# Two linear-attention mixers: elementwise work given to GpSimd, the second substitution put between the first merges, the last grams one step early

## The chip, the cores and the metric

The kernel runs on one core of a Trainium2 chip. The metric is the device time of one execution, in microseconds. Before the change the median of three runs is 3515.9 us (3514.63 to 3524.79).

## What is computed

Two transformer blocks of two layers each, on one sequence of 512 tokens of width 1024, in fp32. Each layer of the first block has a feed-forward part, a mixer and another feed-forward part. The mixer splits one projection into sparse attention, an RWKV-7 recurrence (4 heads of 64) and a gated delta rule (4 heads of 64). The change lies in the last two. The delta rule in its chunked form, which fixes the order of its work:

```python
decay = jnp.exp(jnp.where(incl, g[..., :, None] - g[..., None, :], -jnp.inf))
kb = k * beta[..., None]
lower = jnp.where(strict, jnp.einsum('bhncd,bhnsd->bhncs', kb, k) * decay, 0.0)
rhs = jnp.concatenate([v * beta[..., None], kb * jnp.exp(g)[..., None]], axis=-1)
sol = lax.linalg.triangular_solve(jnp.eye(C) + lower, rhs, left_side=True, lower=True, unit_diagonal=True)
# per chunk, with u, wk = the halves of sol and intra = the masked q k^T * decay
v_new = uc - wc @ S
o = (qc * exp(gc)) @ S + ac @ v_new
S = S * exp(g_last) + (kc * exp(g_last - gc)).T @ v_new
```

The RWKV recurrence is brought to the same form: a unit lower triangular matrix per block and head is inverted, then the state is carried from block to block.

## The kernel before

Everything is written out by hand, engine by engine, with semaphores. Weights come as 128x1024 tiles over a ring of four (SyncE loads them; ScalarE rounds a tile to its high part, line 738; GpSimd makes the low part by four subtractions of 128x256, line 695; TensorE multiplies in three passes, lines 2231 to 2233). GpSimd does nothing else but this, in the order of the tiles (`low_parts`, line 698), apart from a cast near the end.

The mixer, once per layer (`recurrences` of each engine): 512 tokens are four blocks (TB = 4) of 128. In a block, four heads of RWKV and four of the delta rule lie side by side, so a matrix per head and block is a tile of 2 units x 512 columns (1024 columns). It goes as follows.

1. Under the attention of the same layer, VectorE and ScalarE prepare gates, decays and the convolution. Its end is the start of what matters here. VectorE adds the decay mask to four blocks of four heads (line 1755, 16 instructions), ScalarE takes SiLU and squares of keys and queries (lines 1044, 1045), TensorE sums the squares (line 2378), ScalarE takes roots (929), VectorE inverts and widens them (1539, 1541), and TensorE spreads them over the partitions (2385). Ten and then five matmuls of 128 columns without use (2519, 2524) stand around the sums.
2. VectorE scales the keys (1804) and multiplies them by beta (1805), TensorE makes the first block's grams (2640), and VectorE masks them (`take_grams`, 1835 and 1836). Then VectorE finishes the attention output (1775), v times beta (1815), the small diagonal blocks (`small_blocks`, 1847 to 1850) and the query scaling (1818). TensorE turns ten units (2604), and ScalarE copies them out (1076).
3. The inverse. VectorE inverts the 16x16 diagonal blocks by substitution: 15 steps of three dependent instructions, a shuffle and two tensor_tensor (lines 1859 to 1861), on 8 to 120 columns. `lower_corners` (1866) cuts out the part of the matrix for the first merge, `spread_inverses` (1873 to 1878) lays the small inverses out. TensorE and VectorE or ScalarE then merge 16 to 32, 32 to 64 and 64 to 128 (levels 4, 5, 6; TensorE lines 2677, 2679, 2689, 2691, 2695; `merge16` on VectorE, 1892 and 1893).
4. `core_step(l, n)` for n = 0 to 4 does the merges of block n and the recurrence of block n-1: grams with the state's inputs (`a_grams`, 2640, masked in 1903 to 1907), right sides R (2716 to 2722), new values U by the inverse (`writes`, 2731), outputs and the new state (2738 to 2758; `next_state` on VectorE, 1917 to 1923). VectorE runs the substitution of block n+1 in step n, after the merges at level 4 of block n:

```python
                if n < TB:
                    dve.wait_ge(S["small_ready"], b + 1)
                    for g in range(2):
                        merge16(g)
                if n + 1 < TB:
                    lower_corners(n + 1)
                    substitute(range(15, 0, -1))
                    spread_inverses(l, n + 1)
                if 0 < n < TB:
                    next_state()
```

Each engine's queue is in order, so a waiting instruction holds everything behind it. TensorE's order in a step is: gram n+1, level 4 products, `a_grams`, level 4 inverse products, level 5 products, right sides, and so on. After step 4 `post` goes on with the output projection, for which four weight tiles are ready since before the mixer.

## Time and profile before

| | |
|---|---|
| runs (3) | 3515.9 us median, 3514.63 to 3524.79 |
| the profiled execution | 3516.75 us, its span 3514.9 us |
| busy in the span | TensorE 96%, VectorE 41%, ScalarE 36%, GpSimd 48% |
| mean granted clock of TensorE | 0.981 |
| GpSimd idle in the mixers | 564 to 783 us and 1728 to 1954 us |
| first mixer's core | from 615 us (attention's end) to 770 us (output projection) |
| second mixer's core | from 1786 us to 1940 us |

Of the rows below, a timeline row is: start and length in us, engine, line, operation, output and inputs, shape, number of merged instructions, and in brackets the idle time before it with what ended it. A row of windows is: stretch and length, busy time (with the number of instructions) of TensorE, its weight loads, VectorE, ScalarE and GpSimd, then TensorE's granted clock, DMA share and GB/s. Lines are those of the kernel before.

### The profile page before, as it was taken

How to read it: one execution, taken by the hardware profiler on the slowest of the kernel's cores; microseconds unless marked ns; L12 is line 12 of the kernel's file. 1: busy time of each engine (PE TensorE's matmuls, PEld its weight loads, DVE VectorE, ACT ScalarE, POOL GpSimd, SP SyncE). 2: the span in 40 equal slices, each digit the busy share in tenths (PEclk: the TensorE clock that was granted, in tenths of full speed). 3: DMA queues.
4: the chain of work that ended last, by engine and by line, in shares of the span. 5: the costliest groups of instructions: out<-in, count | busy, mean ns of one | idle time of the engine just before them, and what ended most of it. 6: DMA issues, size and time to landing. Idle time of an engine off the chain costs nothing.

```text
span 3514.9 us, 47288 instructions
## 1 busy us (share of the span) xinstructions
PE 3377.4 (96%) x16952; PEld 2779.3 (79%) x16952; DVE 1430.3 (41%) x2753; ACT 1254.3 (36%) x1892; POOL 1674.2 (48%) x2052
## 2 busy tenths in 40 slices
PE   7999998799999999999969999999899999999999
PEld 6888776688888888887658888878667888888887
DVE  5431597845221422148786522224563110341100
ACT  4222436424222322234553432233533332433321
POOL 6765552005665566655300366644304555435554
PEclk9999999899999999999989999999999999999999
DMA  5443321003443344333100244332102222212222
GB/s 184 143 144 112 106 94 60 2 7 132 143 143 114 125 143 144 123 104 96 61 25 2 87 146 144 131 103 84 66 1 84 95 95 96 78 61 102 98 99 96
DMA packets 104224, 340.50 MB, mean 97 GB/s; under 512 B 12144, under 2 KB 17936, under 8 KB 103968
## 3 DMA queue, kind: packets, MB, share of 16 engines
q1 hardware_dynamic: 87824, 283.08, 24.2%
q10 hardware_dynamic: 16272, 55.65, 4.8%
q8 instruction: 88, 1.44, 0.2%
q14 instruction: 40, 0.33, 0.0%
HBM read 330.78 MB, written 2.65 MB: 95 GB/s over the span
## 4 chain that ended last, share of the span: by engine, by line
issue 38%; POOL 33%; PE 27%; DVE 1%; POOLq 0%; ACT 0%; DMA 0%; SPq 0%; DVEq 0%
POOL w_lo L695 33%; PE ps L2233 7%; PE ps L2231 7%; PE ps L2232 7%; PE ps L3003 1%; PE ps L2982 1%; PE ps L2254 0%; PE ps L2991 0%; PE ps L2255 0%; PE ps L2259 0%; PE ps L3093 0%; DVE stat L2132 0%; DVE sq L2125 0%; PE ps L3099 0%; PE ps L2983 0%
## 5 line engine op out<-in xcount | busy, mean ns | idle before, releaser
L695 POOL TENSOR_TENSOR w_lo<-w_raw,w_hi 128x256 fp32r<-128x256 f32 x2040 | 1667.5, 849 | 1823.2 <-ACT w_hi L738 1817.0
L2231 PE MATMUL ps<-h_hi,w_hi 128*128 128x512 f32 x2608 | 1020.7, 391 | 0.9 <-ACT mem L955 0.9
L2233 PE MATMUL ps<-h_hi,w_lo 128*128 128x512 f32 x2608 | 1016.3, 390 | 0.0
L2232 PE MATMUL ps<-h_lo,w_hi 128*128 128x512 f32 x2608 | 1015.9, 390 | 0.0
L738 ACT ACTIVATE w_hi<-w_raw 128x1024 fp32r<-128x1024 f32 x510 | 538.5, 1058 | 916.8 <-DMA w_raw<-in_tiles 916.5
L2231 PEld LDWEIGHTS ps<-h_hi,w_hi 128*128 128x128 f32 x2608 | 490.0, 188 | 112.8 <-issue 6.1
L2233 PEld LDWEIGHTS ps<-h_hi,w_lo 128*128 128x128 f32 x2608 | 490.0, 188 | 102.6
L2232 PEld LDWEIGHTS ps<-h_lo,w_hi 128*128 128x128 f32 x2608 | 490.2, 188 | 100.6
L2232 PE MATMUL ps<-a_lo,w_hi 128*128 (+1 forms) x1120 | 437.2, 390 | 0.0
L2231 PE MATMUL ps<-a_hi,w_hi 128*128 (+1 forms) x1056 | 411.0, 389 | 0.0
L2233 PE MATMUL ps<-a_hi,w_lo 128*128 (+1 forms) x1056 | 411.0, 389 | 0.0
L881 ACT ACTIVATE sil<-ps 128x512 f32<-128x512 f32 x128 | 76.5, 598 | 694.5 <-PE ps L2233 686.3
L1474 DVE TENSOR_TENSOR sil<-sil,ps 128x512 f32<-128x512 f32 x128 | 88.0, 688 | 530.5 <-ACT sil L881 530.5
L1476 DVE TENSOR_TENSOR a_lo<-sil,a_hi 128x512 f32 (+1 forms) x132 | 93.9, 711 | 495.2 <-ACT a_hi L889 495.2
L2232 PEld LDWEIGHTS ps<-a_lo,w_hi 128*128 128x128 f32 x1120 | 211.1, 188 | 43.9
L2231 PEld LDWEIGHTS ps<-a_hi,w_hi 128*128 128x128 f32 x1056 | 198.3, 188 | 41.2
L2233 PEld LDWEIGHTS ps<-a_hi,w_lo 128*128 128x128 f32 x1056 | 198.2, 188 | 40.9
L1453 DVE SCALAR_TENSOR_TENSOR ada_raw<-ada_raw,sq 128x1024 f32<-128x1024 f32 x96 | 164.8, 1720 | 11.1 <-DMA ada_raw<-in_ada_tiles 11.1
L1507 DVE SCALAR_TENSOR_TENSOR x<-ps,x 128x512 f32<-128x512 f32 x32 | 22.1, 692 | 311.5 <-PE ps L2233 311.0
L1507 DVE SCALAR_TENSOR_TENSOR x<-ps,ada,x 128x512 f32<-128x512 f32 x16 | 12.0, 751 | 193.3 <-PE ps L2233 193.2
L889 ACT ACTIVATE a_hi<-sil 128x512 f32 (+1 forms) x132 | 81.2, 615 | 1.6 <-DVE sil L1471 1.6
L2254 PE MATMUL ps<-h_hi,w_hi 128*128 128x512 f32 x176 | 72.1, 410 | 5.1 <-ACT h_hi L839 5.1
(470 smaller groups left out, 3616.9 us busy)
## 6 DMA issues: line engine op xcount, KB each, us to landing
w_raw<-in_tiles SPq DMA_DIRECT2D x510, 512.0 KB, 3.3
ada_raw<-in_ada_tiles ACTq DMA_DIRECT2D x96, 512.0 KB, 3.3
mem<-mem SPq DMA_DIRECT2D x80, 64.0 KB, 2.1
x<-in_x_t SPq DMA_DIRECT2D x2, 1024.0 KB, 6.5
sq<-in_cond ACTq DMA_DIRECT2D x4, 512.0 KB, 4.0
mem<-gates SPq DMA_DIRECT2D x8, 256.0 KB, 3.8
consts<-in_consts SPq DMA_DIRECT2D x1, 1280.0 KB, 12.7
core_mem<-gates SPq DMA_DIRECT2D x8, 128.0 KB, 2.9
```

The costliest lines, as they stand in the source:

```text
L695: ins = nc.gpsimd.tensor_tensor(w_lo[:, s, part], w_raw[:, s, part], w_hi[:, s, part].bitcast(F32), ALU.subtract)
L738: nc.scalar.activation(w_hi[:, t % RING, :], w_raw[:, t % RING, :], ACT.Copy).then_inc(S["w_hi_ready"], 1)
L881: nc.scalar.activation(sil[:, j, :], ps[:, 2 * j, :], ACT.Silu).then_inc(S["silu_ready"], 1)
L889: nc.scalar.activation(a_hi[:, 2 * i + j, :], sil[:, j, :], ACT.Copy).then_inc(S["a_hi_ready"], 1)
L1453: nc.vector.scalar_tensor_tensor(raw, raw, 1.0, cond_rows(n)[0], ALU.mult, ALU.mult, accum_out=ada[:, 0, column]).then_inc(S["ada_used"], 1)
L1474: nc.vector.tensor_tensor(sil[:, j, :], sil[:, j, :], ps[:, 2 * j + 1, :], ALU.mult).then_inc(S["af_ready"], 1)
L1476: nc.vector.tensor_tensor(a_lo[:, 2 * i + j, :], sil[:, j, :], a_hi[:, 2 * i + j, :].bitcast(F32), ALU.subtract).then_inc(S["a_ready"], 1)
L2231: nc.tensor.matmul(bank, wh, hi, start=first, stop=False, skip_group_check=True)
L2232: nc.tensor.matmul(bank, wh, lo, start=False, stop=False, skip_group_check=True)
L2233: return nc.tensor.matmul(bank, wl, hi, start=False, stop=last, skip_group_check=True)
L2254: nc.tensor.matmul(ps[:, banks[r], :], w_hi[:, slot, block], h_hi[:, k, :], start=(n == 0), stop=False, skip_group_check=True)
L2982: nc.tensor.matmul(ps[:, 2 * (i % 2), :], q, kmla[0:QKD, h, 0:T], start=True, stop=True)
```

## The change

GpSimd gets, per layer, in `delta_parts`: the decay masks of blocks 1 to 3 (two adds of 128x512 each; block 0 stays on VectorE), keys times decay, v times beta, the query scaling, queries and keys times the decay factor (with a separate negation), and `lower_corners` of all four blocks (each 128x1024). This stands in its queue between the low part of the last tile loaded ahead of the mixer and that of the next. ScalarE gives the squares to VectorE, splits its exponential in two and copies the spread query factors out of PSUM, scaled. TensorE's head sums move behind the attention's last products, and the five matmuls of line 2524 go. The two halves of the spread inverses are signalled apart. In step 0, VectorE runs six steps of block 1's substitution, then the first merge, one step, the second merge, eight steps. The masking of the small blocks is rearranged so that it works on half as many columns. The grams of the last block's recurrence move: two of them into step 3, two behind the right sides of step 4.

```diff
+            def delta_parts(l):
+
+                pool.wait_ge(S["g_taken"], l + 1)
+                pool.wait_ge(S["dt_spread"], 64 * (l + 1))
+                for n in range(1, TB):
+                    at = ST_GNEG + 4 * n
+                    decay = mem[:, 20 + n, :].rearrange("p (a b t) -> p a b t", a=2, b=2)
+                    g = stat[:, at:at + 4].rearrange("p (b a) -> p a b", b=2).unsqueeze(3).to_broadcast([P, 2, 2, P])
+                    nc.gpsimd.tensor_tensor(heads(mem[:, 20 + n, :]), heads(mem[:, 20 + n, :]), over_heads(const("decay_neg")), ALU.add).then_inc(S["gdn_parts"], 1)
+                    pool.wait_ge(S["gdn_parts"], 10 * l + 2 * n - 1)
+                    nc.gpsimd.tensor_tensor(decay, decay, g, ALU.add).then_inc(S["gdn_parts"], 1)
+                pool.wait_ge(S["spread_taken"], 3 * l + 3)
+                pool.wait_ge(S["eg_ready"], 4 * l + 2)
+                nc.gpsimd.tensor_tensor(mem[:, 24:26, :], mem[:, U_KG:U_KG + 2, :], mem[:, U_DELTA:U_DELTA + 2, :], ALU.mult).then_inc(S["gdn_parts"], 1)
+                pool.wait_ge(S["conv_act_v"], 3 * l + 3)
+                nc.gpsimd.tensor_tensor(mem[:, 37:39, :], mem[:, 37:39, :], core_mem[:, R_SQ:R_SQ + 2, :], ALU.mult).then_inc(S["gdn_parts"], 1)
+                lower_corners(l, 0)
+                pool.wait_ge(S["turned_out"], 11 * l + 1)
+                q = mem[:, U_QG:U_QG + 2, :]
+                nc.gpsimd.tensor_tensor(q, q, sil[:, :, :], ALU.mult).then_inc(S["gdn_parts"], 1)
+                pool.wait_ge(S["turned"], 11 * (l + 1))
+                pool.wait_ge(S["gdn_parts"], 10 * l + 9)
+                eg, qe, kbe = (mem[:, u:u + 2, :] for u in (41, 37, 24))
+                nc.gpsimd.tensor_tensor(qe, q, eg, ALU.mult)
+                nc.gpsimd.tensor_scalar(kbe, mem[:, 39:41, :], -1.0, None, ALU.mult).then_inc(S["gdn_parts"], 1)
+                pool.wait_ge(S["gdn_parts"], 10 * l + 10)
+                nc.gpsimd.tensor_tensor(kbe, kbe, eg, ALU.mult).then_inc(S["gdn_ready"], 1)
+                for n in range(1, TB):
+                    lower_corners(l, n)
+
+            def lower_corners(l, n):
+
+                b = TB * l + n
+                pool.wait_ge(S["gram_taken"], 2 * b + 2)
+                if n == 0:
+                    pool.wait_ge(S["gdn_parts"], 10 * l + 8)
+                else:
+                    pool.wait_ge(S["dx_ready"], merge_turn(b - 1, 4, 1) + 1)
+                nc.gpsimd.tensor_tensor(all_heads(core_mem[:, C_N:C_N + 2, :]), all_heads(lower_units(n)), const("levels").unsqueeze(1).to_broadcast([P, 8, P]), ALU.mult).then_inc(S["corners_ready"], 1)
+
...
+                ahead = BASE[f"mix_out{l}"] + RING
+                low_parts(done, ahead)
+                delta_parts(l)
+                done = ahead
...
-                        for at, unit in ((2, U_KG), (0, U_QG)):
-                            link(nc.scalar.activation(mem[:, unit:unit + 2, :], core_mem[:, G_CONV + at:G_CONV + at + 2, :], ACT.Silu))
-                            nc.scalar.activation(mem[:, U_NORMED + at:U_NORMED + at + 2, :], mem[:, unit:unit + 2, :], ACT.Square).then_inc(S["head_sq"], 1)
-                        load_sqrt()
-                        head_roots(2, 2, 1.0, EPS_NORM, 2)
+                        nc.scalar.activation(mem[:, U_KG:U_KG + 2, :], core_mem[:, G_CONV + 2:G_CONV + 4, :], ACT.Silu).then_inc(S["conv_act_v"], 1)
...
+                nc.scalar.activation(mem[:, U_QG:U_QG + 2, :], core_mem[:, G_CONV:G_CONV + 2, :], ACT.Silu).then_inc(S["conv_act_v"], 1)
+                load_sqrt()
+                head_roots(2, 2, 1.0, EPS_NORM, 2)
+                factors_out()
                 head_roots(3, 2, 1.0, EPS_NORM)
                 act.wait_ge(S["spread_taken"], 3 * l + 2)
-                nc.scalar.activation(mem[:, 20:24, :], mem[:, 20:24, :], ACT.Exp).then_inc(S["dt_ready"], 1)
+                nc.scalar.activation(mem[:, 20, :], mem[:, 20, :], ACT.Exp).then_inc(S["eg_ready"], 1)
+                act.wait_ge(S["gdn_parts"], 10 * l + 6)
+                nc.scalar.activation(mem[:, 21:24, :], mem[:, 21:24, :], ACT.Exp).then_inc(S["eg_ready"], 1)
...
+                act.wait_ge(S["turned"], due("turned"))
+                nc.scalar.activation(sil[:, :, :], ps[:, 2:4, :], ACT.Copy, scale=HD ** -0.5).then_inc(S["turned_out"], 1)
...
+                for h in range(4):
+                    block = mem[:, 20, blk(2 * (h % 2) + h // 2)]
+                    ins = V.scalar_tensor_tensor(block, block, stat[:, ST_GNEG + h:ST_GNEG + h + 1], const("decay_neg"), ALU.add, ALU.add)
...
+                for x, (at, unit) in enumerate(((2, k), (0, q))):
+                    dve.wait_ge(S["conv_act_v"], 3 * l + x + 1)
+                    V.tensor_tensor(mem[:, U_NORMED + at:U_NORMED + at + 2, :], unit, unit, ALU.mult).then_inc(S["head_sq"], 1)
...
+                dve.wait_ge(S["eg_ready"], 4 * l + 2)
+                V.tensor_copy(block_columns(ST_EGL), by_block(eg)[:, :, :, P - 1])
+                fresh_rows()
+                head_inverse(mem[:, U_NORMED + 2:U_NORMED + 4, :], 2, 2)
+                outputs(TB * 8 * (l + 1))
+                dve.wait_ge(S["y_att_out"], TB * (l + 1))
...
-                dve.wait_ge(S["eg_ready"], 2 * l + 2)
-                V.tensor_copy(block_columns(ST_EGL), by_block(eg)[:, :, :, P - 1])
-                V.tensor_tensor(mem[:, 24:26, :], k, mem[:, U_DELTA:U_DELTA + 2, :], ALU.mult).then_inc(S["kd_ready"], 1)
...
+                head_inverse(mem[:, U_NORMED:U_NORMED + 2, :], 2)
+                dve.wait_ge(S["eg_ready"], 4 * l + 3)
                 take_grams(l, 0)
-                outputs(TB * 8 * (l + 1))
-                dve.wait_ge(S["y_att_out"], TB * (l + 1))
-                dve.wait_ge(S["conv_act_v"], l + 1)
-                V.tensor_tensor(mem[:, 37:39, :], mem[:, 37:39, :], beta, ALU.mult).then_inc(S["head_done"], 1)
                 small_blocks(l, 0)
-                dve.wait_ge(S["head_spread"], due("head_spread"))
-                V.scalar_tensor_tensor(q, q, HD ** -0.5, ps[:, 2:4, :], ALU.mult, ALU.mult).then_inc(S["head_done"], 1)
-                due("head_done", 2)
...
+                    blocks = all_heads(lower_units(n)[rows])[:, :, rows]
+                    ins = V.scalar_tensor_tensor(C_M16[rows], blocks[:, :, 16:32], HALF32[rows, 1:2], blocks[:, :, 0:16], ALU.mult, ALU.add)
                 link(ins)
-                V.tensor_tensor(C_M16, C_M32[:, :, 0:16], C_M32[:, :, 16:32], ALU.add)
-                link(V.tensor_copy(C_Y16, EYE16.unsqueeze(1).to_broadcast([P, 8, 16])))
+                link(V.tensor_tensor(C_M16, C_M16, STRICT16.unsqueeze(1).to_broadcast([P, 8, 16]), ALU.mult))
...
+                if TB * l + n:
+                    dve.wait_ge(S["diagonal_spread"], TB * l + n)
...
-                quarter = QUARTER.unsqueeze(1).unsqueeze(3).to_broadcast([P, 8, 4, 32])
-                V.tensor_tensor(spread(inv_units(n)), C_X32.unsqueeze(2).to_broadcast([P, 8, 4, 32]), quarter, ALU.mult).then_inc(S["small_ready"], 1)
+                quarter = QUARTER.unsqueeze(1).unsqueeze(3).to_broadcast([P, 4, 4, 32])
+                for g in range(2):
+                    V.tensor_tensor(spread(inv_units(n)[:, g:g + 1, :]), C_X32[:, 4 * g:4 * g + 4, :].unsqueeze(2).to_broadcast([P, 4, 4, 32]), quarter, ALU.mult).then_inc(S["small_ready"], 1)
+                if n + 1 < TB:
+                    fresh_rows()
...
                 if n == 0:
-                    dve.wait_ge(S["turned"], 10 * (l + 1))
-                    V.tensor_tensor(mem[:, 37:39, :], mem[:, U_QG:U_QG + 2, :], mem[:, 41:43, :], ALU.mult)
-                    V.scalar_tensor_tensor(mem[:, 24:26, :], mem[:, 39:41, :], -1.0, mem[:, 41:43, :], ALU.mult, ALU.mult).then_inc(S["gdn_ready"], 1)
-                if n:
-                    a_grams()
+                    dve.wait_ge(S["small_ready"], 2 * b + 2)
+                    substitute(range(15, 9, -1))
+                    merge16(0)
+                    substitute(range(9, 8, -1))
+                    merge16(1)
+                    substitute(range(8, 0, -1))
+                if 0 < n < TB:
+                    a_grams(n, range(4))
                 if n == TB:
+                    a_grams(n, (2, 3))
                     for k in range(4):
...
+                if 0 < n < TB:
+                    dve.wait_ge(S["small_ready"], 2 * b + 2)
                     for g in range(2):
                         merge16(g)
+                if 0 < n < TB - 1:
+                    substitute(range(15, 0, -1))
                 if n + 1 < TB:
-                    lower_corners(n + 1)
-                    substitute(range(15, 0, -1))
+                    if n == 0:
+                        dve.wait_ge(S["gdn_ready"], l + 1)
                     spread_inverses(l, n + 1)
+                if n == TB - 1:
+                    a_grams(TB, (0, 1))
                 if 0 < n < TB:
                     next_state()
...
-                        for at, bank in ((2, 2), (0, 3)):
-                            pe.wait_ge(S["head_sq"], due("head_sq"))
-                            head_sums(mem_units(U_NORMED + at, U_NORMED + at + 1), bank, at).then_inc(S["head_sum"], 1)
-                        for _ in range(5):
-                            nc.tensor.matmul(ps[:, 1, 0:P], const("ident"), const("ones"), start=True, stop=True)
-                        pe.wait_ge(S["head_inv"], due("head_inv"))
-                        for c in range(2):
-                            head_spread(mem[:, U_NORMED + 2 + c, :], c).then_inc(S["head_spread"], 1)
...
                     if at == 6:
-                        pe.wait_ge(S["head_done"], due("head_done"))
+                        pe.wait_ge(S["gdn_parts"], 10 * l + 7)
                     if at == 8:
-                        pe.wait_ge(S["kd_ready"], l + 1)
+                        pe.wait_ge(S["gdn_parts"], 10 * l + 8)
...
+                    if lev == 4:
+                        pe.wait_ge(S["small_ready"], 2 * b + g + 1)
+                        pe.wait_ge(S["corners_ready"], b + 1)
...
+                    if lev == 4:
+                        pe.wait_ge(S["diagonal_spread"], b + 1)
...
+                    if b > 1:
+                        pe.wait_ge(S["y_out"], b - 1)
+                    if n == 1:
+                        pe.wait_ge(S["gdn_parts"], 10 * l + 9)
+                    if n == TB:
+                        return
                     if n + 1 < TB:
                         pe.wait_ge(S["gram_taken"], 2 * b + 4)
                     elif n > 1:
                         pe.wait_ge(S["s_out"], b)
-                    if b > 1:
-                        pe.wait_ge(S["y_out"], b - 1)
...
-                    pe.wait_ge(S["a_gram_out"], 4 * b)
+                    pe.wait_ge(S["a_gram_out"], 4 * b - 2 if n == TB else 4 * b)
...
+                    if n == TB - 1:
+                        grams(LAST_BANKS, "a_gram_ready", ((kt, ap), (kt, rt)), n)
+                    if n == TB:
+                        grams(LAST_BANKS, "a_gram_ready", ((nb, rt), (kg, qg)), last)
...
+                    if n >= TB - 1:
+                        pe.wait_ge(S["a_gram_out"], 4 * b + 2 if n < TB else 4 * b)
```

## Rows read from the trace of the kernel before

**Rows 1.** Windows of the first mixer's core, all engines.

```profile
644.00:648.00 4.00, 0.00 (x0) 0.00 (x0) 3.52 (x18) 0.00 (x0) 0.00 (x0) 0.50 0.01 2
...
669.00:675.00 6.00, 0.00 (x0) 0.00 (x0) 5.45 (x21) 1.71 (x4) 0.00 (x0) 0.84 0.00 0
...
675.00:679.00 4.00, 3.96 (x18) 3.76 (x20) 3.36 (x10) 0.76 (x2) 0.00 (x0) 0.50 0.00 0
...
758.00:762.00 4.00, 4.00 (x20) 3.89 (x20) 2.30 (x4) 0.00 (x0) 0.00 (x0) 0.57 0.00 0
...
762.00:770.00 8.00, 6.63 (x51) 5.96 (x51) 0.00 (x0) 1.56 (x4) 0.00 (x0) 0.79 0.00 0
```

**Rows 2.** TensorE's timeline in the first mixer.

```profile
622.18 2.48 PE L2524 MATMUL ps<-consts 128*128 128x128 f32 x10
...
624.46 1.47 PE L2385 MATMUL ps<-consts,mem 128*128 128x128 f32 x8
...
639.55 1.16 PE L2640 MATMUL ps<-mem 64*128 64x128 f32 x16 [0.69 <-ACT mem L1076]
...
651.39 3.75 PE L2677 MATMUL ps<-core_mem 128*128 128x128 f32 x16 [10.68 <-DVE core_mem L1878]
...
675.04 3.75 PE L2677 MATMUL ps<-mem,core_mem 128*128 128x128 f32 x16 [6.25 <-DVE mem L1878]
...
727.42 0.61 PE L2758 MATMUL ps<-core_mem,sil 128*64 128x128 f32 x8
...
729.04 2.02 PE L2677 MATMUL ps<-mem,core_mem 128*128 128x128 f32 x16 [1.02 <-ACT mem L1154]
...
758.00 0.46 PE L2716 MATMUL ps<-state,mem 128*128 128x128 f32 x2 [1.95 <-issue]
```

**Rows 3.** TensorE's timeline in the second mixer.

```profile
1821.78 3.75 PE L2677 MATMUL ps<-core_mem 128*128 128x128 f32 x16 [10.62 <-DVE core_mem L1878]
```

**Rows 4.** VectorE's timeline in the first mixer.

```profile
615.98 4.29 DVE L1755 SCALAR_TENSOR_TENSOR mem<-mem,stat,consts 128x128 f32<-128x128 f32 x16 [0.58 <-DMA mem<-gates]
...
631.71 1.22 DVE L1815 TENSOR_TENSOR mem<-mem,core_mem 128x1024 f32<-128x1024 f32 x1
...
632.85 1.70 DVE L1847 TENSOR_TENSOR mem<-core_mem,masks 32x256 f32<-32x256 f32 x4
...
635.04 1.22 DVE L1818 SCALAR_TENSOR_TENSOR mem<-mem,ps 128x1024 f32<-128x1024 f32 x1
...
647.95 1.22 DVE L1866 TENSOR_TENSOR core_mem<-core_mem,consts 128x1024 f32<-128x1024 f32 x1
...
650.02 1.23 DVE L1878 TENSOR_TENSOR core_mem<-mem,masks 128x1024 f32<-128x1024 f32 x1
...
652.61 1.71 DVE L1847 TENSOR_TENSOR mem<-sq,masks 32x256 f32<-32x256 f32 x4
...
659.54 0.41 DVE L1893 TENSOR_TENSOR core_mem<-core_mem,ps 128x256 f32<-128x256 f32 x1
...
702.05 0.61 DVE L1923 SCALAR_TENSOR_TENSOR state<-state,stat,consts 128x128 f32<-128x128 f32 x2
...
753.03 0.61 DVE L1923 SCALAR_TENSOR_TENSOR state<-state,stat,consts 128x128 f32<-128x128 f32 x2
```

**Rows 5.** Source line 695: columns are count, shortest/median/longest ns, first and last start.

```profile
L695 POOL TENSOR_TENSOR w_lo<-w_raw,w_hi x2040: 717/738/2474, 13.3 to 3497.0; 128x256 fp32r<-128x256 f32 x186
```

**Rows 6.** GpSimd's timeline in the second block, 2480 to 2489 us.

```profile
2481.87 5.67 POOL L695 TENSOR_TENSOR w_lo<-w_raw,w_hi 128x256 fp32r<-128x256 f32 x8 [8.19 <-ACT w_hi L738]
```

**Rows 7.** VectorE's timeline in the same stretch.

```profile
2483.53 0.63 DVE L2060 TENSOR_TENSOR mem<-mem 128x64 f32<-128x64 f32 x1
...
2487.73 0.22 DVE L2060 TENSOR_TENSOR mem<-mem 128x64 f32<-128x64 f32 x1
```

**Rows 8.** GpSimd's groups by form: busy us, mean ns, idle before.

```profile
L695 POOL TENSOR_TENSOR w_lo<-w_raw,w_hi 128x256 fp32r<-128x256 f32 x2040 | 1667.5, 849 | 1823.2 <-ACT w_hi L738 1817.0
...
L3275 POOL MEMSET const-float32-1.0<- 128x1 f32 x1 | 0.1, 98 | 0.0
```

More of the change, by code:

```diff
@@ L266, in build_program, with a_unit, a_bank @@
         C_R, C_U = sil[:, 0, :], sil[:, 1, :]
+        LAST_BANKS = (1, 7)
+        def a_unit(n, g):
+            return g if n == TB and g < 2 else C_A + g
+        def a_bank(n, g):
+            return LAST_BANKS[g % 2] if n == TB else (0, 1, 6, 7)[g]
         HALF = T // 2
@@ L292, in all_heads @@
             return units.rearrange("p u (h t) -> p (u h) t", h=4)
-        BLOCK16, EYE16, QUARTER, EIGHTH, HALF32 = (masks[:, at:at + w] for at, w in ((0, 32), (32, 16), (48, 4), (52, 8), (60, 2)))
+        STRICT16, EYE16, QUARTER, EIGHTH, HALF32 = (masks[:, at:at + w] for at, w in ((0, 16), (32, 16), (48, 4), (52, 8), (60, 2)))
         def merge_turn(b, lev, g):
@@ L711, in _ @@
+            cosines = BASE["dft_time"]
+            done = 0
+            for l in range(DEPTH):
+                ahead = BASE[f"mix_out{l}"] + RING
+                low_parts(done, ahead)
+                delta_parts(l)
+                done = ahead
+            low_parts(done, cosines + 2)
             pool.wait_ge(S["w_used"], BASE["dft_group"])
@@ L1750, in attention @@
                 dve.wait_ge(S["g_taken"], l + 1)
-                for n in range(TB):
-                    for h in range(4):
-                        at = ST_GNEG + 4 * n + h
-                        block = mem[:, 20 + n, blk(2 * (h % 2) + h // 2)]
-                        ins = V.scalar_tensor_tensor(block, block, stat[:, at:at + 1], const("decay_neg"), ALU.add, ALU.add)
+                for h in range(4):
+                    block = mem[:, 20, blk(2 * (h % 2) + h // 2)]
+                    ins = V.scalar_tensor_tensor(block, block, stat[:, ST_GNEG + h:ST_GNEG + h + 1], const("decay_neg"), ALU.add, ALU.add)
                 ins.then_inc(S["spread_taken"], 1)
@@ L1893, in merge16, with a_grams @@
                     V.tensor_tensor(odds(inv_t, 4), odds(inv_t, 4), compact(ps[:, 4 + g, half[1]], 4), ALU.add).then_inc(S["merged16"], 1)
-                def a_grams():
+                def a_grams(n, kinds):
                     pair = lambda ap: ap.rearrange("p (h t) -> p h t", h=2)
@@ L1899, in a_grams @@
                     decay = mem[:, 20 + n - 1, :]
-                    for g in range(4):
-                        dve.wait_ge(S["a_gram_ready"], 4 * (b - 1) + g + 1)
-                        out, src = cm[:, C_A + g, :], ps[:, (0, 1, 6, 7)[g], :]
+                    for g in kinds:
+                        dve.wait_ge(S["a_gram_ready"], 4 * (TB * l + n - 1) + g + 1)
+                        out, src = cm[:, a_unit(n, g), :], ps[:, a_bank(n, g), :]
                         V.tensor_tensor(pair(out[:, half[0]]), pair(src[:, half[0]]), both("strict" if g < 2 else "incl"), ALU.mult)
@@ L1924, in next_state @@
                     ins.then_inc(S["s_out"], 1)
+                if n == 0:
+                    dve.wait_ge(S["eg_ready"], 4 * l + 4)
                 if n + 1 < TB:
@@ L2608, in recurrences @@
             def recurrences(l):
+                for at, bank in ((2, 2), (0, 3)):
+                    pe.wait_ge(S["head_sq"], due("head_sq"))
+                    head_sums(mem_units(U_NORMED + at, U_NORMED + at + 1), bank, at).then_inc(S["head_sum"], 1)
+                pe.wait_ge(S["head_inv"], due("head_inv"))
+                for c in range(2):
+                    head_spread(mem[:, U_NORMED + 2 + c, :], c).then_inc(S["head_spread"], 1)
                 pe.wait_ge(S["spread_taken"], 3 * l + 3)
@@ L2718, in right_sides @@
                             at = P * c + HD * hh
-                            nc.tensor.matmul(ps[:, 6, at:at + HD], cm[:, C_A + hh, blk(c)], tm(v_t[c], hh), start=False, stop=hh == 1)
+                            nc.tensor.matmul(ps[:, 6, at:at + HD], cm[:, a_unit(n, hh), blk(c)], tm(v_t[c], hh), start=False, stop=hh == 1)
                     for c in range(2):
@@ L2749, in outputs @@
                             rows = slice(HD * hh, HD * hh + HD)
-                            nc.tensor.matmul(out_y(2, c, rows), tm(v_t[c], hh), cm[:, C_A + hh, blk(2 + c)], start=False, stop=False)
+                            nc.tensor.matmul(out_y(2, c, rows), tm(v_t[c], hh), cm[:, a_unit(n, hh), blk(2 + c)], start=False, stop=False)
                     for c in range(2):
```

37 lines of the change are left out of this document (12 added, 25 removed).

## The prediction

> **What bounds the kernel now.** I first read the windows of the first mixer's core. TensorE, busy 96% of the whole span, stands still there: nothing in 644 to 648, nothing in 669 to 675, and after each pause it runs at half clock (granted 0.50 in 675 to 679, 0.57 in 758 to 762, 0.79 in 762 to 770), which is its 1.2 GHz level instead of 2.4 [rows 1]. Then TensorE in order of time: the first products of the triangular inverse (L2677) start at 651.39 although the gram before them began at 639.55; those of block 1 start at 675.04; the last step's right sides (L2716) start at 758.00 [rows 2]. The second mixer repeats all this 1170.4 us later [rows 3]; two mixers pay or gain alike. VectorE's timeline says what TensorE waits for: substitutions of 45 small dependent instructions, from the end of L1818 (636.3) to L1866 (647.95), 11.7 us, and before and behind each of them work of full width [rows 4]. GpSimd is idle in the mixers (from 564 to 783 us in the first, by the table of the profile), so its time is free. Its port is the question.
>
> **The change without sharing, per mixer.**
> (a) Up to the first L2677. Five filler matmuls (2.48 us, L2524) ahead of the key spread go; TensorE first ends the query sums, so the spread starts about 1.6 earlier than 624.46 [rows 2]. On VectorE, between gram and substitution, the attention output (half of L1815's width, so 0.6), L1815 (1.2) and L1818 (1.2) leave; the four L1847 (1.70 with 256 columns) become four of 128 columns, for which L1755 pays 4.29/16 = 0.27: 0.6 saved [rows 4]. Sum 3.6. Behind the substitution L1866 leaves (1.2), and L1878 is cut in two, of which TensorE needs the first: 0.5. Together 1.6+3.6+1.7 = 6.9, start at 644.5. Moved to ScalarE (query scaling, 1 us) and VectorE (two squares, 1.2 each, formerly ScalarE's): these sit in front of the root that the keys wait for anyway, at no gain and a loss under 0.3.
> (b) Up to block 1. VectorE now does from 644.5: second half of the spreading and fresh rows 0.8, grams 1.4 (from L1878's end 651.2 to L1847 at 652.61), small blocks 1.5, substitution 11.7, two merges 1.5 (four instructions of L1893's 0.41), spreading 1.6 (from L1866's end, 649.1, to L1878, and half of L1878) [rows 4]. That is 663.0; TensorE's own gram before it ends at 663.8. Against 675.04 that is 11.2. The second merge ends at 654.2 instead of 659.95: it is held back by the substitution steps in front of it, TensorE waits there, and that is in the count.
> (c) Block 1. The 6 us pause is gone, so the clock stays up: half of 4 us at 0.50 and a little behind it, 2.4; one L1866 less fresh rows, 0.8. State written (702.05+0.61 = 702.66 before) after 14.4 saved [rows 4].
> (d) Block 2 gains nothing: TensorE ends it itself (L2758 to 728.0, ScalarE's copy, L2677 at 729.04) [rows 2].
> (e) Block 3 gets a gram of 1.1 on TensorE. Step 4 starts its right sides at the state (753.03+0.61 = 753.6) and not at 758.00: 4.4, less 0.5 for the gram now in the shadow of ScalarE's copy of R. With no pause its clock stays: 0.43 of 4 us and 0.21 of 6.6 busy us, 3.1.
> Sum: 14.4-1.1+3.9+3.1 = 20.3 us a mixer, 40.6 in all.
>
> **The price: one SBUF port.** VectorE's small two-input instructions in the second block, with GpSimd splitting weights beside them, took 0.63 us for 128x64 where the same took 0.22 a little later without it; GpSimd did its eight pieces back to back in 5.67 meanwhile, 0.70 each [rows 5 to 7]. So each such VectorE instruction waits for the GpSimd instruction that is running, GpSimd takes the next turn, and VectorE pays. The other way one GpSimd piece grew from 0.72 to 2.47 [rows 5]. Instructions with a PSUM operand I take as exempt.
> The new GpSimd instructions are 512 and 1024 columns long and not 256. Fixed cost 0.1 (a memset of one column), 0.64 per 256 columns [rows 5, 8]: 1.35 for 512, 2.65 for 1024, taken as 2.6; the negation, with one input, as 1.1. Bounds for 1024: 1.2 (VectorE's own time, L1815) and 3.5 (four pieces at the mean, 0.85 each [rows 8], rounded up). Per mixer: 6 masks, 9 products of 1024 (kd, v-beta, q, qe, kbe, four corners) and the negation.
> Waits on VectorE's chain. Masks from 616.0, in turn with VectorE's four mask instructions and two squares: 4 waits of 1.1 before the key squares, one before the copy of the root, about 5.0. The head sums then meet a TensorE that has paused 4 us: 1.5 for its clock (0 to 3). From the keys on kd, v-beta, corners, q, qe, negation, kbe follow each other without a gap, and VectorE has a two-input instruction ready behind every one: waits of about 1.9 (copy of the query root, partly under TensorE's gram), 0.9, 2.4, 2.3 (small blocks), 2.4, 0.7, 2.1 (substitution): 12.7. Corners 1, 2 and 3 each fall into a substitution: 1.8+1.6, and the third's 1.6 in block 2, where TensorE's chain hides 1.4 of it: 3.6. Sum 5.0+1.5+12.7+3.6 = 22.8.
> Net +2.5 a mixer, +5 in all. The profiled execution took 3516.75, 0.85 above the median of the runs, 3515.9; on the median 3521.
>
> The Trainium skill (SBUF — State Buffer, on the shared port pair) says that the port is locked for the whole instruction and that the loser fully blocks. The row has this for instructions of 0.7 us alone; no run here shows it for 2.6. By the rule the sum is the one above; without it, the first rival. The Trainium skill (GPSIMD Engine Reference, Performance versus the Vector engine) gives 4497 ns for a two-input instruction of 2048 columns; an estimate from it is 2.3 us for 1024, by which the sum would be 5 us lower. No run here shows that either.
>
> **Hidden work and new waits.** ScalarE now waits for the last mask before its second Exp, and behind that wait stand its SiLUs, the query scaling and the ten copies of turned units, for which TensorE waits before gram 1. The masks end near 626, so these copies end near 645, 18 us before the first L2677; without that cover each late microsecond would count. TensorE's turned units 6 and 8 wait for kd and v-beta (636 and 639), inside the same cover. VectorE waits for kbe before it spreads block 1, because that spreading writes over the decay factors: 651 against 681. TensorE's outputs in steps 3 and 4 wait for the new masking of the last grams, 1.3 us on a VectorE that is idle in step 3 and works under the 1.9 us of writes in step 4. Corners 0 (needed by TensorE with the first L2677) end some 20 us ahead of it; kbe and qe end 30 us before block 1. GpSimd's split of mixer-output tile 4 now stands behind all this; it waited for ScalarE until 783, the last corners end near 722. No DMA is issued or moved. If GpSimd took twice as long, corners 0 would still be hidden.
>
> **Rivals.** (1) The port comes back within a long instruction, say every 256 columns: VectorE's waits shrink to 0.6, the price falls by about 10 a mixer, less what was hidden: -7.5 a mixer, **3501**; with no waits at all 3475. For: nothing longer than 0.7 us has been seen on GpSimd. Against: the other direction (2.47) held for a whole long VectorE instruction. Chance 0.25, half of it near 3475.
> (2) Slower: GpSimd takes longer per column with broadcast or split operands (masks, corners), which none of its instructions in this trace has. At 3.5 and 1.75 each wait behind a long one grows by 0.9 and each mask wait by 0.4, nine and five of them: 10 a mixer, **3540**. It decides from about 2.9 us per 1024 columns. For: the row's mean is already 0.85 per piece. Against: that mean holds waits; the median is 0.74. Chance 0.14.
> (3) The edits do not matter, because TensorE's own chain replaces each wait: 3516. Against it, TensorE is idle for 10.7 and 6.3 us. Chance 0.03.
> The forecast has 0.58, its own range 3500 to 3538: 0.08 of it lies below, 0.38 within and 0.12 above 0.3% (10.5 us, about what a measurement of this kernel can tell). Faster 0.08+0.25 = 0.33; same 0.38+0.03 = 0.41; slower 0.12+0.14 = 0.26. The range reaches from between the two forms of rival 1 (3484) to rival 2 (3538).
>
> **What the profile would show.** Right: GpSimd's masks and products at 1.3 and 2.4 to 2.7 us, VectorE's small L1860-like instructions at 0.2 except some five per mixer at 2 to 3; the first L2677 near 663 and not 644; block 1 near 684; no TensorE pause ahead of it, clock 1.0 in it; right sides directly behind the state; outputs ending near 772 and 1942. Wrong on the port: no VectorE instruction in the substitution above 0.9, first L2677 near 645 to 652, end near 749 to 762. Wrong on GpSimd's speed: products at 3 us and more, ends near 780. Wrong on the last step: L2716 more than 1 us behind the state, or its clock near 0.5, worth 3 a mixer.

## The result and the profile after

The changed kernel takes **3531.5 us** (median, 3529.0 to 3532.4), the kernel before 3515.5 beside it (3510.7 to 3524.8): a ratio of **1.0043, 95% interval 1.0033 to 1.0052**, 16 us slower. The forecast was 3521, range 3484 to 3538, with chances of 0.33 for faster, 0.41 for the same and 0.26 for slower, where a change within 0.3% counted as the same. By that line the kernel is slower. The profiled executions are 3529.0 and 3516.75 us, spans 3526.9 and 3514.9.

What GpSimd does in the first mixer (its timeline; rows of before: none, it was idle):

```profile
618.31 1.38 POOL L729 TENSOR_TENSOR mem<-mem,consts 128x512 f32<-128x512 f32 x1 [51.28 <-DMA mem<-gates]
...
634.25 2.35 POOL L734 TENSOR_TENSOR mem<-mem 128x1024 f32<-128x1024 f32 x1 [6.65 <-DVE mem L1871]
636.67 2.70 POOL L736 TENSOR_TENSOR mem<-mem,core_mem 128x1024 f32<-128x1024 f32 x1
639.51 2.36 POOL L759 TENSOR_TENSOR core_mem<-core_mem,consts 128x1024 f32<-128x1024 f32 x1
...
646.24 2.34 POOL L744 TENSOR_TENSOR mem<-mem 128x1024 f32<-128x1024 f32 x1 [2.01 <-PE ps L2665]
648.64 2.77 POOL L745 TENSOR_SCALAR mem<-mem 128x1024 f32<-128x1024 f32 x1
651.48 2.34 POOL L747 TENSOR_TENSOR mem<-mem 128x1024 f32<-128x1024 f32 x1
```

Products of 1024 columns take 2.34 to 2.70 us, with broadcast operands (L759) no more than without. VectorE's timeline in the same stretch, with the masks (L1814), the copies of the last decay columns (L1863) and of the query root (L1602), a masked gram (L1891), the small blocks (L1902) and instructions of the substitution:

```profile
618.19 4.03 DVE L1814 SCALAR_TENSOR_TENSOR mem<-mem,stat,consts 128x128 f32<-128x128 f32 x4 [0.82 <-DMA mem<-gates]
...
625.27 1.23 DVE L1863 COPY stat<-mem 128x8 f32<-128x8 f32 x1
...
634.37 2.78 DVE L1602 COPY mem<-head_tok 128x1024 f32<-128x1024 f32 x1
...
637.07 0.41 DVE L1891 TENSOR_TENSOR core_mem<-ps,consts 128x256 f32<-128x256 f32 x1
...
638.51 6.24 DVE L1902 SCALAR_TENSOR_TENSOR mem<-core_mem,masks 32x128 f32<-32x128 f32 x4
...
646.37 0.18 DVE L1918 STREAM_SHUFFLE mem<-mem 128x24 f32<-128x24 f32 x1
646.58 2.05 DVE L1919 TENSOR_TENSOR mem<-mem 128x24 f32<-128x24 f32 x1
648.66 1.04 DVE L1920 TENSOR_TENSOR mem<-mem 128x24 f32<-128x24 f32 x1
...
649.97 0.19 DVE L1919 TENSOR_TENSOR mem<-mem 128x32 f32<-128x32 f32 x1
...
651.62 2.27 DVE L1920 TENSOR_TENSOR mem<-mem 128x48 f32<-128x48 f32 x1
```

In the substitution, the two of over 2 us each end with a GpSimd product: 646.58 + 2.05 = 648.63 against 646.24 + 2.34 = 648.58. The one of 1.04 us stands beside the start of the negation (L745), and those behind it take 0.19 while the negation still runs by the profile. Four masks of 128 columns took 4.29/4 = 1.07 before [rows 4]. So two-input products hold the port as forecast. TensorE, which answers to [rows 2]:

```profile
663.34 3.78 PE L2746 MATMUL ps<-core_mem 128*128 128x128 f32 x16 [15.33 <-DVE core_mem L1935]
...
669.99 1.06 PE L2766 MATMUL ps<-core_mem 128*128 128x64 f32 x8
672.11 1.10 PE L2748 MATMUL ps<-core_mem 128*128 128x64 f32 x8 [1.06 <-DVE core_mem L1952]
674.71 1.97 PE L2748 MATMUL ps<-core_mem 128*128 128x64 f32 x8 [1.50 <-DVE core_mem L1952]
676.47 1.92 PE L2762 MATMUL ps<-core_mem 128*128 128x64 f32 x8
...
768.98 0.49 PE L2791 MATMUL ps<-state,mem 128*128 128x128 f32 x2 [0.76 <-ACT mem L1215]
```

and the windows with the granted clock, for [rows 1], the last of them block 0 of the second mixer:

```profile
core 0: us, PE busy (x) PEld busy (x) DVE busy (x) ACT busy (x) POOL busy (x), PEclk, DMA share, GB/s
663.00:673.00 10.00, 8.60 (x56) 8.47 (x56) 9.12 (x41) 2.01 (x5) 1.80 (x1) 0.76 0.01 2
...
677.00:690.00 13.00, 13.00 (x80) 12.07 (x80) 6.31 (x26) 5.36 (x17) 0.00 (x0) 0.50 0.00 1
770.00:778.00 8.00, 7.31 (x79) 6.64 (x78) 3.82 (x8) 2.34 (x5) 0.00 (x0) 1.00 0.00 0
...
1839.95:1866.51 26.56, 26.56 (x145) 25.73 (x145) 18.77 (x80) 7.12 (x21) 2.35 (x1) 0.51 0.00 1
```

The first row of the timeline stands where the forecast had it, though everything had come 2.25 us later before that. The rest of block 0 does not: eight products of L2748 and L2762 that take 1.1 us at full clock take 1.97 after two gaps (1.06 and 1.50 us) in which TensorE waited for the merges; from 677 to 690 it is busy without a break at clock 0.50, and VectorE (6.31 busy of 13) waits for it. In the second mixer block 0 is at half clock throughout (0.51) and takes as long, 26.56 us, but there TensorE has no gap: it is busy without a break from the first product on, behind a wait of 15.3 us. Block 1 starts at 689.8 (forecast: near 684) and the outputs end at 777.7 and 1955.1 (forecast: near 772 and 1942). At the end of the mixer, right sides follow 0.76 us behind ScalarE's copy, at clock 1.00, as forecast.

To compare kernels I measure from the end of the last score reduction of the attention on VectorE (613.40 before, 615.65 after) to the first products of blocks 0 to 3 and to the last output products of step 4; first mixer, with the whole of the second behind it:

| us | to block 0 | 0 to 1 | 1 to 2 | 2 to 3 | 3 to end | whole | 2nd mixer |
|---|---|---|---|---|---|---|---|
| before | 37.99 | 23.65 | 28.85 | 25.15 | 40.27 | 155.91 | 155.50 |
| after | 47.69 | 26.48 | 28.15 | 24.89 | 34.67 | 161.88 | 163.19 |
| e_tiny | 31.54 | 24.12 | 26.46 | 24.89 | 34.67 | 141.68 | 143.30 |
| e_split | 41.86 | 26.36 | 27.69 | 24.89 | 34.67 | 155.47 | 155.70 |
| e_vec | 39.71 | 27.89 | 26.99 | 26.47 | 34.68 | 155.74 | 154.21 |
| e_nolace | 46.56 | 22.75 | 30.11 | 25.63 | 34.67 | 159.72 | 161.91 |
| e_grams | 37.79 | 23.85 | 28.97 | 25.09 | 34.64 | 150.34 | 149.82 |
| e_filled | 36.75 | 23.29 | 27.04 | 26.47 | 34.68 | 148.23 | 146.47 |

The mixers make 6.0 + 7.7 of the 12.0 us between the spans; 2.25 came before the first, and the stretches between and behind them were 1.0 and 2.9 shorter. The medians differ by 16; where the other 4 us lie, no trace shows.

### The profile page after: what moved, and what is told of

Same layout as the page of the kernel before. It is cut to its first block, busy times and chain, and to the rows that moved or that the text cites. A ratio compares the mean times of both kernels' runs of the same rounds, so it can differ in the third digit from the quotient of the medians.

```text
span 3526.9 us, 47128 instructions
## 1 busy us (share of the span) xinstructions
PE 3389.5 (96%) x16932; PEld 2792.9 (79%) x16932; DVE 1449.2 (41%) x2723; ACT 1252.9 (36%) x1892; POOL 1741.0 (49%) x2084
## 4 chain that ended last, share of the span: by engine, by line
PE 72%; issue 11%; POOL 8%; DVE 7%; ACT 1%; DMA 1%; POOLq 0%; SPq 0%; DVEq 0%; ACTq 0%
PE ps L2300 19%; PE ps L2302 19%; PE ps L2301 19%; POOL w_lo L707 8%; PE ps L2323 1%; PE ps L2324 1%; PE ps L2328 1%; PE ps L2766 1%; PE ps L3082 1%; DMA w_raw<-in_tiles 1%; PE ps L2447 1%; PE ps L2377 1%; DVE mem L1640 1%; PE ps L2706 1%; PE ps L2378 1%
## 6 DMA issues: line engine op xcount, KB each, us to landing
consts<-in_consts SPq DMA_DIRECT2D x1, 1280.0 KB, 12.7
```

## Experiments

Each kernel was timed five to twelve times, beside the kernel before, whose medians were 3516.1 to 3517.0.

**1. GpSimd's instructions cut to a column or two (e_tiny).**

```diff
-nc.gpsimd.tensor_tensor(mem[:, 24:26, :], mem[:, U_KG:U_KG + 2, :], ...
+nc.gpsimd.tensor_tensor(mem[:, 24:26, 0:1], mem[:, U_KG:U_KG + 2, 0:1], ...
```

> The changed kernel with GpSimd's ten wide instructions of a mixer cut to one or two columns, all waits and signals kept (its results are left out: decay masks, decayed keys, beta values, query scaling and corners are not made; TensorE reads other units of the same size in their place). Port theory (VectorE waits for whole GpSimd instructions, 20 us a mixer or more): the waits of 2 to 6 us on VectorE vanish, block 0 starts near 645; with the clock loss of block 0 (4 to 6 us a mixer) still there 3485 to 3492, without it 3475. Rival (the interleaving and the late clock cost the time, not the port): 3520 or more.

3487.9 us (ratio 0.9911, 0.9897 to 0.9924). VectorE's mask group, copy, small blocks, the same step of the substitution and the spreading of block 1's inverses (L1935), and TensorE behind them:

```profile
618.21 1.14 DVE L1814 SCALAR_TENSOR_TENSOR mem<-mem,stat,consts 128x128 f32<-128x128 f32 x4 [0.42 <-DMA mem<-gates]
...
628.54 0.69 DVE L1602 COPY mem<-head_tok 128x1024 f32<-128x1024 f32 x1
...
632.03 1.45 DVE L1902 SCALAR_TENSOR_TENSOR mem<-core_mem,masks 32x128 f32<-32x128 f32 x4
...
635.32 0.18 DVE L1919 TENSOR_TENSOR mem<-mem 128x24 f32<-128x24 f32 x1
...
665.31 1.29 DVE L1935 TENSOR_TENSOR mem<-mem,masks 128x512 f32<-128x512 f32 x2
...
671.59 0.42 DVE L1891 TENSOR_TENSOR core_mem<-ps,consts 128x256 f32<-128x256 f32 x1 [4.85 <-PE ps L2706]
```
```profile
647.30 3.78 PE L2746 MATMUL ps<-core_mem,consts 128*128 128x128 f32 x16 [6.56 <-DVE core_mem L1935]
...
656.10 1.10 PE L2748 MATMUL ps<-core_mem 128*128 128x64 f32 x8 [0.97 <-DVE core_mem L1952]
...
660.96 1.97 PE L2762 MATMUL ps<-core_mem 128*128 128x64 f32 x8
```

This is the change without its price: 14.2 us faster than before in the first mixer, 12.2 in the second. The price of sharing is the rest, 161.88 - 141.68 = 20.2 in the first (19.9 in the second): 16.2 up to block 0, 2.4 and 1.7 in blocks 0 and 1. Block 0's clock falls here too, behind gaps of 0.97 and 0.32 us. VectorE has spread block 1's first inverses by about 666.0, 18.7 us behind block 0's start, and then stands idle for 4.85 us until TensorE's gram of block 0's stage is done: TensorE alone keeps block 1 until 671.42.

**2. The same work in pieces of 256 columns (e_split).**

```diff
-nc.gpsimd.tensor_tensor(q, q, sil[:, :, :], ALU.mult).then_inc(S["gdn_parts"], 1)
+for x in range(4):
+    ins = nc.gpsimd.tensor_tensor(q[:, x // 2, cut(x)], q[:, x // 2, cut(x)], sil[:, x // 2, cut(x)], ALU.mult)
+ins.then_inc(S["gdn_parts"], 1)
```

> The changed kernel with each GpSimd instruction of the mixers cut into pieces of 256 columns. Port theory with the hold lasting one instruction: a VectorE wait shrinks from up to 2.3 us to about 0.7, about 8 us a mixer less than the changed kernel, 3512 to 3518. Rival (what counts is GpSimd's busy time beside VectorE, or GpSimd's results coming late): 3530 or, by ten extra fixed costs, 3535.

3513.0 us (0.9989, 0.998 to 0.9998): 18 below the changed kernel, about level with the kernel before. GpSimd and VectorE:

```profile
644.21 2.77 POOL L757 TENSOR_TENSOR mem<-mem 128x256 f32<-128x256 f32 x4
```
```profile
635.82 2.67 DVE L1922 SCALAR_TENSOR_TENSOR mem<-core_mem,masks 32x128 f32<-32x128 f32 x4
...
646.40 0.65 DVE L1940 TENSOR_TENSOR mem<-mem 128x48 f32<-128x48 f32 x1
```

GpSimd takes longer for the same columns (2.77 for 2.34), VectorE waits oftener, but no instruction of its substitutions takes over 0.7. So the length of one instruction counts, and not GpSimd's busy time, which grew.

**3. All of it back on VectorE (e_vec).**

```diff
+V.tensor_tensor(mem[:, 24:26, :], k, mem[:, U_DELTA:U_DELTA + 2, :], ALU.mult).then_inc(S["gdn_parts"], 1)
...
+lower_corners(l, 1)
```

> The changed kernel with all that GpSimd makes in the mixers back on VectorE, at the places of the kernel before; the four smaller edits (interleaved merges, smaller block preparation, half-wise spreading, last grams a step early, no five filler products) stay. Port theory: 20.3 us a mixer less 9.6 of instructions that VectorE keeps, less some 3 for the clock: 5 to 11 us a mixer faster than before, 3494 to 3506. Rival (the clock loss of the interleaving eats the small edits): 3512 to 3518.

3515.0 us (0.9996, 0.9987 to 1.0005). A miss: nothing was gained, as its rival had it, and block 0 even starts 1.7 later than before. Two causes are read from the rows and were not tried apart (VectorE, then TensorE):

```profile
619.31 4.29 DVE L1775 SCALAR_TENSOR_TENSOR mem<-mem,stat,consts 128x128 f32<-128x128 f32 x16 [0.32 <-DMA mem<-gates]
623.51 2.35 DVE L1822 TENSOR_TENSOR mem<-mem 128x1024 f32<-128x1024 f32 x2
```
```profile
630.22 1.95 PE L2434 MATMUL ps<-consts,mem 128*128 128x128 f32 x8
...
667.42 3.67 PE L2728 MATMUL ps<-core_mem 128*128 128x64 f32 x16 [3.54 <-DVE core_mem L1926]
```

The two squares, moved from ScalarE, now stand behind all 16 masks; the key spread starts 13.6 us behind the reference point and not 11.1 (624.46 in [rows 2]), although the five fillers are gone. And the interleaved merges leave TensorE 3.54 us idle, with clock 0.62 over block 0.

**4. Both merges ahead of the substitution (e_nolace).**

```diff
-substitute(range(15, 9, -1))
 merge16(0)
-substitute(range(9, 8, -1))
 merge16(1)
-substitute(range(8, 0, -1))
+substitute(range(15, 0, -1))
```

> The changed kernel with both first merges of block 0 ahead of the whole substitution of block 1 and not between its steps. Clock theory (two idle gaps of 1.1 and 1.5 us from the interleaving let TensorE fall to half clock for the rest of block 0): granted clock near 1.0 in 667 to 680, block 0's products at 0.7 and 1.2 us instead of 1.1 and 1.9; VectorE's own work sets the start of block 1, so the end gains only 0 to 4 us a mixer: 3523 to 3531. Rival (the interleaving is worth its place, since VectorE stands idle while it waits for block 0's products): start of block 1 later by 2 to 4 us, 3535 to 3540.

3525.5 us (1.0027, 1.0018 to 1.0036): 6 below the changed kernel. TensorE:

```profile
668.58 2.11 PE L2746 MATMUL ps<-core_mem 128*128 128x64 f32 x16
670.53 1.06 PE L2760 MATMUL ps<-core_mem 128*128 128x64 f32 x8
...
677.21 1.16 PE L2704 MATMUL ps<-mem 64*128 64x128 f32 x16
684.38 3.76 PE L2744 MATMUL ps<-mem,core_mem 128*128 128x128 f32 x16 [6.01 <-issue]
```

The gaps are gone, the products take 1.06 instead of 1.92, and block 0 takes 22.75 instead of 26.48 (23.70 in the second mixer). TensorE's last work ahead of block 1, the gram (L2704), ends 16.7 us behind block 0's start. But the pause of 6 us ahead of block 1 is back, with slow first products behind it: block 1 gives 2.0 back. In the rows of the two mixers the interleaving cost 3.4 of the 6 us.

**5. Fillers ahead of block 0 (e_warm), and in the two gaps (e_fillgap).**

```diff
+for _ in range(44):
+    nc.tensor.matmul(ps[:, 6, 0:P], const("ident"), const("ones"), start=True, stop=True)
 if n < TB:
```

> The changed kernel with 44 filler products of 128x128 on TensorE in its wait ahead of block 0 (10 to 12 us of work in a wait of 13). Clock theory: granted clock 1.0 when block 0 starts, its products at 0.7 and 1.2 us, from its first product to block 1's 22.5 to 23.5 us instead of 26.5, 3 to 4 us a mixer less: 3522 to 3526. Rival (VectorE's shared port alone sets the start of block 1): 3529 to 3532.

3530.3 us (1.0036, 1.0022 to 1.005), no change; the rival holds for this wait. The fillers end 5.34 us ahead of block 0 and the merge gaps stand (0.97, 1.58); block 0 takes 25.9 and 27.6 in the two mixers.

```diff
 if lev == 5:
+    if n == 0:
+        for _ in range((6, 7)[g]):
+            nc.tensor.matmul(ps[:, 6, 0:P], const("ident"), const("ones"), start=True, stop=True)
     pe.wait_ge(S["merged16"], 2 * b + g + 1)
```

> The changed kernel with 6 and 7 filler products of 128x128 (0.23 us each at full clock) on TensorE in the two idle gaps of block 0 where it waits for the interleaved merges (1.06 and 1.50 us in the changed kernel's trace). Clock theory (these two gaps make the clock fall for the rest of block 0): clock 1.0 from block 0's second products on, from its first product to block 1's 22.5 to 23.8 us instead of 26.5, 3 us a mixer less: 3523 to 3527. Rival (the clock of block 0 is set by the long wait ahead of it or by chance, or VectorE sets the start of block 1 anyway): 3529 to 3534.

Median 3520.1 (1.001, 0.9999 to 1.0022), 3 below what was expected, but twelve runs from 3510.0 to 3532.2: the two longest had a mean clock of 0.977, the three shortest 0.982 or 0.983. The windows of block 0 in its two mixers show such a split within one execution:

```profile
663.38:687.19 23.81, 23.65 (x170) 22.98 (x171) 18.83 (x80) 6.72 (x20) 2.36 (x1) 0.74 0.01 2
1835.73:1866.42 30.69, 28.68 (x171) 27.57 (x171) 19.61 (x80) 7.60 (x22) 2.35 (x1) 0.61 0.01 1
```
```profile
1843.05 1.56 PE L2742 MATMUL ps<-consts 128*128 128x128 f32 x12
1846.61 1.97 PE L2751 MATMUL ps<-core_mem 128*128 128x64 f32 x8 [2.00 <-DVE core_mem L1952]
1848.37 3.30 PE L2742 MATMUL ps<-consts 128*128 128x128 f32 x14
```

In the first mixer no gap was left and the clock rose; in the second, fillers ran at full clock, ended 2.0 us too soon, the clock fell, and the second filling took 3.30 instead of 1.78. (L2742 is the fillers' line.) Between the two mixers lie 6.9 us, 2.0 of them the gap itself. In this execution, of 3529.9 us, the second mixer lost what the first had gained (165.9 against 163.2 us in the changed kernel, 159.9 against 161.9); of the faster ones only the higher mean clock is known. So a filled gap went with a higher clock, and fillers of fixed number do not always meet the gap.

**6. The last grams a step early, alone (e_grams).** The edit is the change's own, in the kernel before.

> The kernel before with one part of the change alone: the last grams a step early (first pair of block 3 in the writes of step 3, second pair in those of step 4). The forecast's step (e): 1.1 dearer in step 3, 3.9 and 3.1 cheaper in step 4, together 5.9 us a mixer: 3503 to 3506. Rival (step 4 is held by TensorE's outputs at low clock all the same): 3512 to 3516.

3501.9 us (0.9957, 0.9944 to 0.9971), faster than both and 1.1 below what was expected. TensorE at the right sides of step 4:

```profile
755.33 0.49 PE L2729 MATMUL ps<-state,mem 128*128 128x128 f32 x2 [0.76 <-ACT mem L1162]
```

Block 3 to end takes 34.64 instead of 40.27: 5.6 a mixer, against 5.9 forecast. That is 11.3 of the 14.6 us between the medians; where the rest comes from was not looked into.

**7. With the small edits (e_gsmall), then fillers (e_gswarm).** Small blocks 16 wide and spreading by halves, as in the change; then 40 and 20 fillers ahead of blocks 0 and 1.

> The last one with two more of the small edits on VectorE: small blocks prepared 16 wide, and spreading in two halves, each released by itself; no interleaving, nothing moved between engines. VectorE's chain ahead of blocks 0 and 1 gets about 1 us shorter each: 1 to 2.5 us a mixer less than the last grams alone, 3498 to 3503. Rival (the ends are set by the clock of TensorE, not by VectorE): no gain over the last grams alone, 3503 to 3506.

> The kernel before with last grams early and the two small edits, and 40 filler products on TensorE in its wait ahead of block 0 and 20 in that ahead of block 1. Clock theory: no slow stretch at the starts of blocks 0 and 1, 2 to 3 us a mixer less than the same without fillers: 3494 to 3499, the fastest version so far that computes everything. Rival (fillers come late into the wait and delay the products, or the clock falls all the same): 3500 or more.

3500.4 (0.9956, 0.9943 to 0.997) and 3503.9 (0.9963, 0.995 to 0.9977): no gain over the last grams alone, and a miss for the fillers. In the second, block 0 starts at full clock (its first products take 2.05 us) and reaches the merges too early:

```profile
658.49 2.00 PE L2701 MATMUL ps<-core_mem 128*128 128x64 f32 x16 [1.40 <-DVE core_mem L1910]
...
663.10 1.97 PE L2715 MATMUL ps<-core_mem 128*128 128x64 f32 x8
```

In the first, the two mixers differ with no gap in either, which the clock theory did not have:

```profile
651.70:678.61 26.91, 26.91 (x145) 26.09 (x145) 21.10 (x83) 7.47 (x22) 0.00 (x0) 0.50 0.00 1
1814.96:1837.56 22.60, 16.68 (x145) 15.89 (x145) 20.33 (x82) 7.33 (x21) 0.00 (x0) 0.88 0.00 1
```

**8. Merges ahead of two VectorE products (e_late), and with fillers (e_latewarm, e_filled).** Query scaling by decay and decayed beta keys (2.4 us) go behind the merges.

```diff
-if n == 0:
-    V.tensor_tensor(mem[:, 37:39, :], mem[:, U_QG:U_QG + 2, :], mem[:, 41:43, :], ALU.mult)
 for g in range(2):
     merge16(g)
+if n == 0:
+    V.tensor_tensor(mem[:, 37:39, :], mem[:, U_QG:U_QG + 2, :], mem[:, 41:43, :], ALU.mult)
```

> The version with last grams early and the two small edits on VectorE, and in step 0 query scaling by decay and decayed beta keys (2.4 us on VectorE) behind the two first merges instead of ahead of them. No gap in block 0, so the clock holds in both mixers; VectorE does the same work: 0 to 2 us a mixer less than without this move, 3496 to 3501. Rival (no gap was there to be taken away, 10 us of pause alone decide the clock): 3500 to 3504.

3505.2 (0.997, 0.9959 to 0.9982), a miss, 4.8 above e_gsmall: no gap in block 0, and still clock 0.53 over it; it took 28.1 us in both mixers.

> The last one with 42 and 22 filler products on TensorE in the waits ahead of blocks 0 and 1. Clock theory: the merges now come in time, so TensorE has no gap over 0.5 us in block 0 and keeps clock 1.0 through blocks 0 and 1; block 1 starts where VectorE lets it and runs 2 to 3 us shorter: 3491 to 3497. Rival (fillers bring the gaps back, as in the version with fillers before): 3500 to 3505.

3497.7 (0.9945, 0.9932 to 0.9958), 0.7 above what was expected: the clock is 1.00 over block 0 in both mixers, but the second filling ends 2.9 us early.

> The version with last grams early, the small edits, the merges first in step 0 and filler products, with 43 and 33 fillers in the two waits instead of 42 and 22 (the trace of that version shows the second filling end 2.9 us ahead of block 1, whose first products then take 2.9 and 3.6 us instead of 2.05). Clock theory: no wait over 1 us is left ahead of block 1, its first products take 2.05 us, about 1.5 to 2 us a mixer less: 3493 to 3496, some 20 us below the kernel before. Rival (fillers overrun the wait and push block 1 back, or the clock is lost elsewhere): 3498 to 3503.

**3495.7 us (0.9942, 0.9929 to 0.9956)**, 21 below the kernel before and 36 below the changed one; against the last grams alone the intervals overlap. Windows of its blocks 0 and 1:

```profile
652.30:675.59 23.29, 22.67 (x210) 21.76 (x211) 20.41 (x82) 7.41 (x22) 0.00 (x0) 1.00 0.01 1
675.59:702.60 27.01, 25.08 (x256) 23.71 (x256) 23.17 (x95) 9.58 (x25) 0.00 (x0) 1.00 0.01 2
```

Both at full clock. With gaps and waits filled, VectorE sets block 1's start, some 23.3 us behind block 0's.

## Why the prediction was right, and where it was not

**Right in direction and on the port, and inside the range; its central figure was 10.5 us too low.** The forecast was a gain of 20.3 and a price of 22.8 a mixer, net 2.5. Measured in the first mixer: a gain of 14.2, a price of 20.2, net 6.0 (7.7 in the second). Part of this is luck: both terms were put too high, by 6.1 and 2.6, and the second error took back part of the first. That block 0 began near 663 was luck in part too: its start moved by 9.7 us against the reference point and not by 12.3, and 2.25 had been lost before.

**(a) Start of block 0 without sharing:** 6.9 forecast, 6.4 measured (37.99 to 31.54). The two squares in front of the root were put at under 0.3; the rows of e_vec suggest that this holds only while the masks are off VectorE.

**(b) Block 0: the step that failed.** It said 19.3 us to block 1, TensorE's own end, without its terms, and with TensorE at full clock behind its waits. The step says itself that TensorE waits for the merges, "and that is in the count": the wait was counted, the clock was not. With GpSimd's work taken out, block 0 took 24.1 us, 4.8 more than forecast, at clock 0.64; in the changed kernel 26.5 at 0.63 and 0.51 (before: 0.86). VectorE's part was right: 18.5 us forecast, 18.7 in e_tiny, where it then waits for TensorE. TensorE's own work is short enough too: in e_nolace, without gaps and mostly at full clock, it was through after 16.7 us. There VectorE, which waited for both merges and once for GpSimd, held the stage for 22.75. So the 19.3 needed interleaving at full clock, and no run had both.

**(c), (d):** 3.2 forecast in block 1, 2.4 measured in e_tiny; block 2 forecast at nothing, 0.3 measured.

**(e) Last step:** 5.9 forecast, 5.6 measured, alone and in the change.

**The price:** products of 1024 were put at 2.6 and took 2.35. Up to block 0 the waits and slow head sums cost 16.2 for 5.0 + 1.5 + 12.7 = 19.2; behind it 4.1 for 3.6. The negation was put at 1.1 us, with a wait of 0.7 behind it. Its row says 2.77, but it held VectorE up for only 0.9 (1.04 instead of 0.18), close to the forecast.

**Rivals.** (1) A port given back within a product falls: waits last as long as the GpSimd product, and cutting the products to 256 columns took 18 us off. By the rule of the Trainium skill (SBUF — State Buffer, shared port pair), the port is locked for the whole instruction. The trace agrees for two-input products: VectorE's instructions of 0.2 us took 2.05 and 2.27 beside GpSimd's 2.34. For the one-input negation it does not: VectorE was let through after about 1.1 of the recorded 2.77 us. (2) Slower broadcast operands fall: 2.35 (L759) against 2.34 (L744). The estimate from the figure of the Trainium skill (GPSIMD Engine Reference, Performance versus the Vector engine), 2.3 us, agrees with this trace too. That the time moved towards rival 2's 3540 has another cause, the half clock of block 0. (3) Not so: the parts add up to 14 and 20 us.

**Not settled.** After a wait of 10 to 15 us ahead of block 0 the clock came back within its first products in some mixers (the kernel before, e_grams, e_gsmall's second, the changed kernel's first) and stayed at half for the whole block in others (the changed kernel's second, e_gsmall's first, both of e_late), with no gap in these. So the interleaving's gaps account for the half clock of the changed kernel's first mixer, and not for that of its second. What decides it was not found out; filling the wait put the clock at 1.0 in both mixers of e_filled and e_latewarm. Also open is why block 2 took 26.1 to 26.5 and not 24.9 us in a number of mixers (the changed kernel's second, the first of e_vec and of e_filled): its first sixteen products took 3.2 to 3.6 us there instead of 2.05.

## What to carry to other kernels

Here, work moved from VectorE to GpSimd cost VectorE up to the length of the GpSimd product each time the two met: 2.35 us for what VectorE does in 1.2. In pieces the same work cost 18 us less, and was still no faster than all of it on VectorE (3513.0 against 3515.0). A wait of TensorE can have two prices, its length and the products behind it at half clock; a forecast that shortens or moves waits must take the clock from the rows again, and look at every mixer: the two of one execution differed. Read each edit of a bundle by itself: one of them (the last grams early) was worth 14.6 us, and the rest of the change lost it and 16 more.
